# 32 tokens of a PEER layer's first tile: up products by gathered rows, and sixteen low halves by copies and adding transfers

## The reference

```python
def peer_ffn(h, peer_wq, peer_keys, peer_u, peer_v):
    q = (ht @ peer_wq).reshape(T, PEER_HEADS, 2, PEER_DH)
    s = jnp.einsum('thpd,hpkd->thpk', q, peer_keys, ...)
    sv, si = lax.top_k(s, PEER_TOPK)
    cand = (sv[..., 0, :, None] + sv[..., 1, None, :])...
    top, pos = lax.top_k(cand, PEER_TOPK)
    eidx = jnp.take_along_axis(cidx, pos, axis=-1)
    g = jax.nn.softmax(top, axis=-1)
    ...
        u = peer_u[ib]
        a = jax.nn.gelu(jnp.einsum('td,thkd->thk', hb, u), approximate=False)
        return jnp.einsum('thk,thkd->td', gb * a, peer_v[ib])
```

## Time and profile before

| | us |
|---|---|
| median of three runs (1609.28 to 1610.99) | 1610.52 |
| the profiled execution, its own time | 1606.33 |
| its span, first to last instruction | 1604.5 |
| PE busy | 1582.9 (99%) |
| DVE busy | 1338.7 (83%) |
| ACT busy | 634.6 (40%) |
| POOL busy | 406.6 (25%) |

### The profile page before, as it was taken

The page is one execution under the profiler, slowest core; times in us unless marked ns, Lnnn a source line. Parts: engine busy times, 40 slices in busy tenths (PEclk is TensorE's granted clock), DMA queues, the critical chain, the costliest instruction groups (busy, mean ns, idle before and its releaser), DMA issues.

```text
span 1604.5 us, 24652 instructions
## 1 busy us (share of the span) xinstructions
PE 1582.9 (99%) x8490; PEld 1382.4 (86%) x8490; DVE 1338.7 (83%) x2533; ACT 634.6 (40%) x978; POOL 406.6 (25%) x343
## 2 busy tenths in 40 slices
PE   8999999999999999999999999999999999999998
PEld 4777678887889999999998888888888888888887
DVE  6899787774899999999678888888888888888876
ACT  5433834235334445554333333333333333333332
POOL 0000001102435200001244334433343333433420
PEclk9999999999999999999999999999999999999999
DMA  9431245753324467868999999999999999999981
GB/s 339 144 106 40 99 165 185 254 185 120 109 82 151 156 208 251 279 227 259 387 413 387 352 345 332 333 360 358 343 331 328 357 356 349 329 326 359 355 312 69
DMA packets 168012, 418.79 MB, mean 261 GB/s; under 512 B 12673, under 2 KB 78337, under 8 KB 167810
## 3 DMA queue, kind: packets, MB, share of 16 engines
q1 hardware_dynamic: 115472, 247.92, 42.4%
q0 software_dynamic: 42960, 156.79, 27.3%
q10 hardware_dynamic: 9506, 13.12, 2.2%
HBM read 375.83 MB, written 41.95 MB: 260 GB/s over the span
## 4 chain that ended last, share of the span: by engine, by line
PE 94%; DVE 3%; ACT 1%; issue 1%; DMA 0%; DVEq 0%; ACTq 0%
PE bank L1575 18%; PE bank L1577 17%; PE bank L1576 17%; PE bank L1921 11%; PE bank L1922 11%; PE bank L1920 11%; PE bank L1899 3%; PE bank L1831 1%; DVE sb_scr L1086 1%; PE bank L1748 1%; PE bank L1607 1%; PE bank L1738 1%; PE bank L1609 1%; PE bank L1608 1%; DVE sb_scr L987 1%
## 5 line engine op out<-in xcount | busy, mean ns | idle before, releaser
L625 ACT ACTIVATE sb_w_hi<-sb_stage 128x1024 fp32r<-128x1024 f32 x324 | 343.2, 1061 | 541.8 <-PE bank L1922 323.7
L973 DVE TENSOR_TENSOR sb_w_lo<-sb_stage,sb_w_hi 128x1024 fp32r<-128x1024 f32 x294 | 359.4, 1224 | 169.8 <-ACT sb_w_hi L625 168.6
L1575 PE MATMUL bank<-sb_act_hi,sb_w_hi 128*128 128x384 f32 (+1 forms) x1408 | 498.1, 354 | 2.9 <-DVE sb_w_lo L973 2.2
L1577 PE MATMUL bank<-sb_act_hi,sb_w_lo 128*128 128x384 f32 (+1 forms) x1408 | 492.7, 350 | 0.0
L1576 PE MATMUL bank<-sb_act_lo,sb_w_hi 128*128 128x384 f32 (+1 forms) x1408 | 492.2, 350 | 0.0
L1922 PE MATMUL bank<-sb_w_hi,sb_mix_lo 128*128 128x512 f32 x768 | 300.1, 391 | 0.0
L1921 PE MATMUL bank<-sb_w_lo,sb_mix_hi 128*128 128x512 f32 x768 | 299.9, 391 | 0.0
L1920 PE MATMUL bank<-sb_w_hi,sb_mix_hi 128*128 128x512 f32 x768 | 298.8, 389 | 0.0
L1575 PEld LDWEIGHTS bank<-sb_act_hi,sb_w_hi 128*128 128x128 f32 x1408 | 264.4, 188 | 23.3 <-issue 4.4
L1576 PEld LDWEIGHTS bank<-sb_act_lo,sb_w_hi 128*128 128x128 f32 x1408 | 264.5, 188 | 17.3 <-issue 0.5
L1577 PEld LDWEIGHTS bank<-sb_act_hi,sb_w_lo 128*128 128x128 f32 x1408 | 264.2, 188 | 15.2
(11 more groups left out here) (244 smaller groups left out, 1814.6 us busy)
## 6 DMA issues: line engine op xcount, KB each, us to landing
sb_stage<-u_dram SPq DMA_DIRECT2D x128, 512.0 KB, 5.5
sb_stage<-v_dram SPq DMA_DIRECT2D x128, 512.0 KB, 6.0
sb_stage<-w_front_dram SPq DMA_DIRECT2D x68, 512.0 KB, 4.4
g_scratch<-sb_scr SPq DMA_DIRECT2D x12, 2048.0 KB, 8.8
sb_scr<-g_scratch SPq DMA_DIRECT2D x32, 768.0 KB, 8.0
sb_scr<-w_ada_dram POOLq DMA_DIRECT2D x32, 512.0 KB, 4.6
a_scratch<-sb_scr ACTq DMA_DIRECT2D x64, 192.0 KB, 4.0
sb_scr<-a_scratch SPq DMA_DIRECT2D x16, 768.0 KB, 11.7
```

Source lines behind the costliest of these rows:

```text
L625: nc.scalar.activation(w_hi[:, slot, :], stage[:, slot, :], ACT.Copy).then_inc(w_round, 1)
L973: nc.vector.tensor_tensor(w_lo[:, slot, :], stage[:, slot, :], w_hi[:, slot, :].bitcast(F32), ALU.subtract).then_inc(w_split, 1)
L1575: nc.tensor.matmul(out, w_hi[:, slot, w], rhs_hi[:, dc, :], start=(i == 0), stop=False)
L1577: last = nc.tensor.matmul(out, w_lo[:, slot, w], rhs_hi[:, dc, :], start=False, stop=(i == len(dcs) - 1))
```

## The change

1. The up product of every u slab leaves out the first NS = 32 tokens: the moving side is 352 columns wide in place of 384. The first 32 columns of the gelu tile are set to 1 once, so that the gates of these tokens can carry the finished product of gate and gelu.
2. The four hot batches of these tokens go; the first turn has 12 batches in place of 16, and the first of the 24 gate writes goes too.
3. The picks of the 32 tokens, 4096 in all, are spread over 128 partitions (four groups of 32 picks). POOL gathers 32 times 128 rows of `peer_u` (4 KB each) into a ring of six, DVE makes 32 dots with the tokens' activations (`sparse_dot`), 20 in the first turn and 12 in the second, ACT takes the gelu in two halves, DVE multiplies by the gates, and POOL adds the 4096 numbers into the zeroed first part of `g_scratch` by 32 indirect transfers.
4. For that, POOL writes zeros into that part early; PE makes, in the loop over m before the query weights, a copy of the 32 tokens in all four partition groups (4 matmuls for each m), DVE copies it from PSUM before top-k, and the index arithmetic of the first tile gets further additions (pieces 3 and 5) and eight small operations (piece 6).
5. The low halves of u0 to u15 are no longer subtracted by POOL: ACT writes the negated rounded slab into `w_lo` (L748 after the change) and a transfer issued by POOL adds the slab itself to it (L657). POOL then reports the split.

```diff
+NS = 32
+NU = ND - NS
+GROUPS = P // NS
+SPICKS = PICKS // GROUPS
+S_ROWS = 6
+S_HALF = SPICKS // 2
+S_FIRST = (1, 10)
+S_UNITS = 9
...
 TURN_BATCHES = TURN_TOKENS // HB
-def share(n, b):
-    return range(n * b // G_UNITS, n * (b + 1) // G_UNITS)
+S_BATCHES = NS // HB
+def batches(it, b):
+    skip = S_BATCHES if it == 0 else 0
+    n = TURN_BATCHES - skip
+    return range(skip + n * b // G_UNITS, skip + n * (b + 1) // G_UNITS)
+def batch_no(it, n):
+    return it * TURN_BATCHES + n - S_BATCHES
+def group_no(it, j):
+    return it * (TURN_TOKENS // 4) + j - NS // 4
+def sparse_dots(u):
+    half = int(u >= S_FIRST[1])
+    k = u - S_FIRST[half]
+    return [S_HALF * half + d for d in range(S_HALF) if 0 <= k == d * S_UNITS // S_HALF]
...
-                            sp.wait_ge(gw_out[i], 16 * ND // TB // 2)
+                            sp.wait_ge(gw_out[i], 16 * (ND // TB // 2 - (i == 0)))
+                        sp.wait_ge(s_out, 16 * SPICKS)
...
             pool.dma_start(keys[:, :, :], keys_d).then_inc(keys_in, 16)
+            nc.gpsimd.memset(zeros, 0.0).then_inc(gz_ok, 1)
+            pool.wait_ge(gz_ok, 1)
+            for k in range(4):
+                pool.dma_start(g_d[8 * k:8 * k + 8, :, 0:1, :].rearrange("a p n m -> p a (n m)"),
+                               zeros.rearrange("p (o m) -> p o m", o=1).to_broadcast([P, 8, P])).then_inc(gz_in, 16)
...
-            with pool.Fori(WQ0 // RING + 1, POOL_LAST // RING) as turn:
+            nc.gpsimd.memset(ga[:, :, 0:NS], 1.0).then_inc(one_ok, 1)
+            with pool.Fori(WQ0 // RING + 1, FRONT // RING) as turn:
                 for slot in range(RING):
                     split_unit(turn * RING + slot, slot)
...
+            def sum_unit(n):
+                pool.wait_ge(w_neg, n - FRONT + 1)
+                pool.dma_start(w_lo[:, n % RING, :], stage[:, n % RING, :].bitcast(F32R), accum_op=ALU.add
+                               ).then_inc(w_sum[n % RING], 16)
+            def sum_done(n):
+                pool.wait_ge(w_sum[n % RING], 16 * ((n - FRONT) // RING + 1))
+                pool.wait_ge(w_split, n)
+                pool.nop(nofuse=True).then_inc(w_split, 1)
+            sum_unit(FRONT)
+            for n in range(FRONT, POOL_LAST):
+                if n + 1 < POOL_LAST:
+                    sum_unit(n + 1)
...
+            def s_pick(d):
+                h, r = divmod(d, SPICKS // PH)
+                return r * PH + h
+            def sparse_gather(d):
+                k = s_pick(d)
+                if d >= S_ROWS:
+                    pool.wait_ge(s_used, d - S_ROWS + 1)
+                pool.indirect_dma_start(s_row[d % S_ROWS], None, u_rows_d,
+                                        bass.IndirectOffsetOnAxis(ap=s_list.bitcast(U32)[:, 0, k:k + 1], axis=0)
+                                        ).then_inc(sg_in[d % S_ROWS], 16)
+            def sparse_add(d):
+                h, r = divmod(d, SPICKS // PH)
+                k = s_pick(d)
+                if r == 0 and h:
+                    pool.wait_ge(s_out, 16 * (SPICKS // PH) * h)
+                pool.indirect_dma_start(g_flat, bass.IndirectOffsetOnAxis(ap=s_list.bitcast(U32)[:, 1, k:k + 1], axis=0),
+                                        s_w[:, d:d + 1], None, compute_op=ALU.add).then_inc(s_out, 16)
+            pool.wait_ge(st_ok, 1)
+            for g in range(GROUPS):
+                pool.dma_start(s_list[g * NS:(g + 1) * NS, :, :],
+                               m_list[0:NS, :, g * SPICKS:(g + 1) * SPICKS]).then_inc(sl_in, 16)
+            pool.wait_ge(sl_in, 16 * GROUPS)
+            pool.wait_ge(gz_in, 64)
+            for d in range(S_HALF + S_ROWS):
+                sparse_gather(d)
+            pool.wait_ge(sw_ok, 1)
+            for d in range(S_HALF):
+                sparse_add(d)
+                if S_HALF + S_ROWS + d < SPICKS:
+                    sparse_gather(S_HALF + S_ROWS + d)
+            pool.wait_ge(sw_ok, 2)
+            for d in range(S_HALF, SPICKS):
...
             nc.scalar.activation(w_hi[:, slot, :], stage[:, slot, :], ACT.Copy).then_inc(w_round, 1)
+            if isinstance(nn, int) and FRONT <= nn < POOL_LAST:
+                nc.scalar.activation(w_lo[:, slot, :], stage[:, slot, :], ACT.Copy, scale=-1.0).then_inc(w_neg, 1)
...
                 act.wait_ge(ks_ok, c + 1)
+                if c == 0:
+                    act.wait_ge(gz_in, 64)
...
-                    nc.scalar.activation(ga[:, k % 2, :], UB[k][:, 0:ND], ACT.Gelu).then_inc(ge_ok, 1)
+                    nc.scalar.activation(ga[:, k % 2, NS:ND], UB[k][:, 0:NU], ACT.Gelu).then_inc(ge_ok, 1)
...
-                    for j in [2 * n + k for n in share(TURN_BATCHES, b) for k in range(2)]:
+                    for half in range(2):
+                        if it * G_UNITS + b == S_FIRST[half] + S_UNITS:
+                            act.wait_ge(s_used, S_HALF * (half + 1))
+                            d = slice(S_HALF * half, S_HALF * (half + 1))
+                            nc.scalar.activation(s_gelu[:, d], s_dot[:, d], ACT.Gelu).then_inc(sd_ok, 1)
...
                         dve.wait_ge(ijt_ok, tt)
                     sums = eights[:, part, :, :].rearrange("p r k -> p (r k)")
                     link(nc.vector.tensor_tensor(sums, rank_eq[:, 0:8 * P], rank_eq[:, 8 * P:16 * P], ALU.add))
+                    if tt == 0:
+                        link(nc.vector.tensor_tensor(rank_eq[:, 0:4 * P], sums[:, 0:4 * P], sums[:, 4 * P:8 * P], ALU.add))
+                        link(nc.vector.tensor_tensor(rank_eq[:, 0:2 * P], rank_eq[:, 0:2 * P], rank_eq[:, 2 * P:4 * P], ALU.add))
+                        link(nc.vector.tensor_tensor(ijw[0][:, part, :], rank_eq[:, 0:P], rank_eq[:, P:2 * P], ALU.add))
...
                     dve.wait_ge(ijw_ok, tt + 1)
+                    i3, j3 = ijw[tt % 2][:, 0, :], ijw[tt % 2][:, 1, :]
+                    if tt == 0:
+                        link(nc.vector.tensor_copy(ranku[:, 0, :], j3))
+                        mark(nc.vector.scalar_tensor_tensor(out=m_list.bitcast(U32)[:, 0, :], in0=i3, scalar=float(NKEY),
+                                                            in1=j3, op0=ALU.mult, op1=ALU.add))
+                        link(nc.vector.tensor_scalar(ranku[:, 1, :], ranku[:, 0, :], 2, None, ALU.logical_shift_right))
+                        mark(nc.vector.tensor_scalar(rstart, j3, float(TB), place, ALU.mult, ALU.add))
...
                         mark(nc.vector.scalar_tensor_tensor(out=idx3[:, 0, :], in0=i3, scalar=float(NKEY),
                                                             in1=j3, op0=ALU.mult, op1=ALU.add))
                         mark(nc.vector.scalar_tensor_tensor(out=idx3[:, 1, :], in0=j3, scalar=float(NKEY),
...
+            for half in range(2):
+                dve.wait_ge(sh2_ok, DC // 2 * (half + 1))
+                nc.vector.tensor_copy(s_h[:, half * 512:half * 512 + 512], UB[2 + half][:, :]).then_inc(sh2_cp, 1)
...
+            def sparse_dot(d):
+                dve.wait_ge(sg_in[d % S_ROWS], 16 * (d // S_ROWS + 1))
+                nc.vector.tensor_tensor_reduce(s_row[d % S_ROWS], s_row[d % S_ROWS], s_h, 1.0, 0.0, ALU.mult, ALU.add,
+                                               s_dot[:, d:d + 1]).then_inc(s_used, 1)
+            def sparse_weights(half):
+                hs = slice(half * PH // 2, (half + 1) * PH // 2)
+                dve.wait_ge(sd_ok, half + 1)
+                dve.wait_ge(sl_in, 16 * GROUPS)
+                nc.vector.tensor_tensor(s_w.rearrange("p (h r) -> p h r", h=PH)[:, hs, :],
+                                        s_list[:, 2, :].rearrange("p (r h) -> p h r", h=PH)[:, hs, :],
+                                        s_gelu.rearrange("p (h r) -> p h r", h=PH)[:, hs, :], ALU.mult).then_inc(sw_ok, 1)
             def g_turn(it, first):
                 weight_parts(it)
                 for b in range(G_UNITS):
                     split_unit(it * G_UNITS + (FRONT + G_FIRST + b + 2), (FRONT + G_FIRST + b + 2) % RING)
-                    for n in share(TURN_BATCHES, b):
+                    for n in batches(it, b):
                         hot_batch(it, n, first)
+                    for d in sparse_dots(it * G_UNITS + b):
+                        sparse_dot(d)
+                    for half in range(2):
+                        if it * G_UNITS + b == S_FIRST[half] + S_UNITS + 1:
+                            sparse_weights(half)
                     if b in PIECE_UNITS:
...
                                         ident).then_inc(ht_ok, 1)
+                    for g in range(GROUPS):
+                        last = nc.tensor.matmul(UB[2 + m // 4][g * NS:(g + 1) * NS, m % 4 * P:(m % 4 + 1) * P],
+                                                wide[:, m, 0:NS], ident, start=True, stop=True)
+                    last.then_inc(sh2_ok, 1)
                 if m >= 2:
...
             for c in range(2, 2 * PH):
+                if c == 2:
+                    pe.wait_ge(sh2_cp, 2)
```

(39 more changed lines are left out.)

36 lines of the change are left out of this document (26 added, 10 removed).

## The result

The changed kernel takes 1625.24 us (median of five runs, 1623.93 to 1625.54) against 1609.48 for the kernel before (1609.13 to 1610.99): a ratio of 1.0099, 95% interval 1.0087 to 1.0111. It is 15.8 us slower. The profiled execution took 1625.46, its span is 1623.2. The forecast was 1611.3, between 1604 and 1625.

A forecast was written before the change was run, and what follows sets the result against it. PE and DVE were both taken as full up to u55, with room on DVE only after u56. Profiled 1606.3 + 23.8 (u56 later) - 23.0 (72 narrower slabs) = 1607.1; median 4.2 higher, 1611.3 us, range 1604 to 1625.

The forecast's parts named there:

- Wrong it is ... if that split starts after 548: Sign against the prediction: DVE's split of u16, forecast near 544 us, starting later than 548.
- PE, narrower products: u slabs on PE: 352-column matmuls take 160.0 ns, saving 0.32 us a slab, 41.0 us over 128 slabs.
- PE, added matmuls: Loop over m before the query weights: 4 extra matmuls per m cost PE 3.0 us, 1.5 as lower end.
- POOL's subtraction goes: Top-k on DVE, u0 to u15: without POOL's lock on two-input adds, 9 us off.
- The adding transfer: u0 to u15: landing of u15 lets DVE start its index section at 544.0 us in place of 546.51.
- D: Time of one 512 KB adding transfer: taken as 7.0 us, lower 4.6, upper end 9.2.
- the ring: Stage slots for u0 to u15 come round every 15.36 us and need 8.1 + D; holds up to D = 7.3.
- Rival 1: Adding transfer slow, D = 9.2: u15 lands 2.2 us later, stage ring short by 5.8 more; 1619 us, chance 0.20.
- Past D = 7.3 each further microsecond costs four: Rule in Rival 1 for the stage ring of u0 to u15: cost of a transfer longer than 7.3 us.
- The rule of the Trainium skill: An adding transfer needs two source reads, about half a copy's rate; would put D at or near its upper end.
- DVE to the last hot batch: From index section start: 248.8 us, 1.0 of it late first rows; last hot batch at 792.8.
- Rival 2: First turns: gathered rows come late, list 2 us and slow issues up to 3 us; 1616 us, chance 0.11.

The follow-up runs named there:

- b_adds_only: The kernel before with only the negated copies and adding transfers for u0 to u15: 1610.40 us, ratio 1.0014.
- a_sub_back: The changed kernel with POOL's subtraction of u0 to u15 back in place of negated copies and adding transfers: 1617.39 us, ratio 1.0052.
- j_wide16: As a_sub_back, but PE's products of u0 to u15 are 384 columns wide again: 1620.62 us, ratio 1.0065.
- d_three: The changed kernel with POOL issuing the adding transfer for u(n+2) before waiting for u(n), three under way, not two: 1630.96 us, ratio 1.0145.
- i_quarter_add: The changed kernel with adding transfers cut to the first 256 of 1024 columns of each slab: 1615.03 us, ratio 1.0033.
- h_free: As a_sub_back, without the 32 row gathers and 32 dots: 1580.20 us, ratio 0.9822.
- e_turn12: As a_sub_back, with every third split of u22 to u55 (11) moved from DVE to ACT's negated copy and an adding transfer: 1644.72 us, ratio 1.0218.

## Why the prediction was wrong

It had the order of events and missed the size: the forecast was +1.8 us to the median of before's new runs, the measured +15.8. In the profiled executions u56 starts 18.1 us later than forecast (812.09 against 794.0). The prediction's own sign, "Wrong it is ... if that split starts after 548", came true at 554.94. By its steps:

- **PE, narrower products: right, in part by luck.** 158.3 ns in place of the 160.0 forecast in u0 to u15 and in the laps, 166.7 in most of the turns, where it doesn't count. The gain after u56 is 23.2 us; forecast 23.0. At 158.3 ns, 72 slabs would give 25.9; 3.3 us of a wait at the first v slab, which the prediction didn't have, take most of the rest.
- **PE, added matmuls: right.** 2.07 us for one m, against 1.50 in the loop of before: 0.57 x 6 = 3.4 us, forecast 3.0.
- **POOL's subtraction goes: right as a number, wrong as a gain.** b_adds_only shows the 9 us. But the price was read from a trace in which POOL works every 4.16 us; with the change's own period of 3.8 it is 3 us (a_sub_back, j_wide16).
- **The adding transfer: the step that failed.** "I take 7.0" measured 8.0, and "8.1 + D. It holds up to D = 7.3, barely" did not hold. The forecast for the index section was 544.0; it began at 554.9. Of these 10.9 us 2.1 were in the execution before anything of the change (the rounding of unit 24 starts at 201.27 in place of 199.13); they may belong to the 4.2 us by which the profiled execution of before lay under its median. 0.4 are the added matmuls, and 8.4 are the landing of u15: 1.2 because the add of u3 is issued late, 6.0 because twelve steps take 4.34 us in place of 3.84, 1.1 for the transfer of u15 itself (8.1), and 0.1.
- **What was missing in the ring.** A slot came round every 17.4 us; the prediction's own sum, with D = 8.0, is 16.1. In the last round (add of u11 issued at 529.19, add of u15 at 546.42) 8.0 us are the transfer, 5.7 the next load, 2.0 ACT's two copies, as forecast; but then 1.5 us pass before POOL issues, where the prediction had 0.5 for handing over:

```profile
543.83 1.04 ACT L748 ACTIVATE sb_w_lo<-sb_stage 128x1024 fp32r<-128x1024 f32 x1
```

POOL is still waiting for the report of u13, behind which the add of u15 stands in its program.
- **Rival 1 named this step, but its size was right by luck.** Its 8 us were worked out for D = 9.2. By its own rule ("Past D = 7.3 each further microsecond costs four") the measured D of 8.0 gives some 3 us, not 8.4.
- **What sets the pace of 4.34 us is open.** Two transfers of 8.0 us under way would give 4.0 us a slab, the ring 4.0 (8.1 + 8.0, over four); both are near 4.34. A third possibility was left untested: that the DMA engines are full. Their share from 494 to 546 us is 1.00 in the changed kernel and 0.56 in the kernel before (the number before the last):

```profile
494.00:546.00 52.00, 49.03 (x292) 47.81 (x290) 48.08 (x345) 30.30 (x38) 10.27 (x12) 0.97 1.00 262
```

```profile
494.00:546.00 52.00, 52.00 (x302) 52.00 (x301) 51.24 (x342) 18.14 (x25) 26.31 (x11) 1.00 0.56 171
```

It is 1.05 in b_adds_only and 0.99 in d_three (to 550 us). i_quarter_add takes all three away at once and so doesn't choose.
- **The rule of the Trainium skill** (Collectives: The Full Stack, "The bandwidth ceiling: the fold count and why AG ≠ RS ≠ AR"), half the rate of a copy, is not seen in a transfer that is alone: that of u0, at 471.62, landed after 4.6 us, as long as a plain one. It is nearly seen in the time of the DMA engines. In the same stretch the adding transfers (q0) and the slab loads (q1) moved (packets, MB, share of the 16 engines):

```profile
q0 software_dynamic: 1589, 5.79, 56.0%
q1 hardware_dynamic: 1535, 5.61, 31.4%
```

For a megabyte the adding transfers took 1.7 times the share of the loads. The prediction had the rule only as a length D; as a load on the engines it was not counted, and it deserved more than a chance of 0.20.
- **DVE to the last hot batch: right for work, short for waits.** 554.94 to 809.55 are 254.6 us, of which 7.2 waits; 247.4 of work against 247.8 forecast. Waits were taken at 1.0: 6 us more. Rival 2 had 5 more, for late first rows. But only 2.8 us are waits for the first rows; 2.6 are for rows whose gathers stand behind indirect additions on POOL's queue, and 1.8 for ACT and PE. That its number fits is again partly luck.
- **u56: 2.5 us** after the last hot batch in place of 1.2. Two batches, 32 small matmuls, stand there and not 16.

So a loss of 8 us and one of 6 us came together, near the sizes of two rivals that each had a chance of its own: 1611.3 + 8 + 5 is 1624. The range was built as if only one could: 1625.0 was its edge, 1625.24 the result. And the balance itself was fragile: with DVE as the bound, these microseconds went to the end, as h_free and i_quarter_add show from the other side.

## What to carry to other kernels

When a change makes an engine the bound, its small terms stop being hidden: sum their upper ends together, not one by one. The cost of the lock between DVE and POOL, two engines that run in rounds, was here the difference of their periods, so it must be worked out with the periods that the change leaves, not read off the trace before. A transfer whose landing others wait for is best put in a queue that has nothing else to wait for; d_three and e_turn12 show the price of the other order. And before transfers are added to a stretch, their time on the DMA engines is to be set against the share that is already taken there.
